# Reading a carried-in state through 128x128 weights: eight matmuls with 8 streamed columns in place of eight with 128 and two gathers

## The reference, cut to what matters

```python
G = jnp.cumsum(blk(g), axis=3)
qg = qc * jnp.exp(G)
kg = kc * jnp.exp(-G)
A = jnp.where(causal, jnp.einsum('bhncd,bhnsd->bhncs', qg, kg), 0.0)
o_intra = jnp.einsum('bhncs,bhnsv->bhncv', A, vc)
...
o_inter = jnp.einsum('bhncd,nbhdv->bhncv', qg, s_prev)
o = (o_intra + o_inter).transpose(0, 2, 3, 1, 4).reshape(b, n * c, H, dv)[:, :L]
```

## Time and profile before

| | |
|---|---|
| median of 3 runs | 2112.25 us (2110.99 to 2112.82) |
| profiled execution, its own time | 2110.99 us |
| its span | 2109.4 us |
| the eight rounds | about 220 us to 900 us of the span, 87 to 88 us each |
| PE busy | 2029.4 us, 96% |
| PE matmul records | 14632 |
| DVE busy | 1047.8 us, 50% |
| ACT busy | 809.1 us, 38% |

### The profile page before, as it was taken

How to read it: one execution, slowest core, us unless ns; L and a number is a source line. 1 busy time by engine, 2 the same in 40 slices (tenths; PEclk the granted TensorE clock), 3 DMA queues, 4 the chain that set the end, 5 groups by cost and what they waited for, 6 DMA issues and landing times.

```text
span 2109.4 us, 38265 instructions
## 1 busy us (share of the span) xinstructions
PE 2029.4 (96%) x14632; PEld 1905.8 (90%) x14632; DVE 1047.8 (50%) x1333; ACT 809.1 (38%) x1068; POOL 74.9 (4%) x119
## 2 busy tenths in 40 slices
PE   7999999999999999879998899999999999999996
PEld 6999878888788788679998899999999999999996
DVE  6344545546555355455445744444444445445445
ACT  5333444434444344244334433333323333445442
POOL 1001010010100101000000000000000000000000
PEclk9999999999999999999999999999999999999998
DMA  7776797988879889865643354444444444443441
GB/s 252 169 239 213 292 346 275 343 301 321 339 283 349 302 309 341 291 225 184 226 160 109 111 170 149 149 148 140 148 150 159 149 149 142 149 149 131 167 139 50
DMA packets 123910, 444.00 MB, mean 210 GB/s; under 512 B 14517, under 2 KB 18645, under 8 KB 123792
## 3 DMA queue, kind: packets, MB, share of 16 engines
q1 hardware_dynamic: 113888, 403.78, 53.6%
q0 software_dynamic: 9968, 39.48, 6.4%
HBM read 423.28 MB, written 22.54 MB: 211 GB/s over the span
## 4 chain that ended last, share of the span: by engine, by line
PE 88%; DVE 6%; ACT 2%; issue 2%; DMA 2%; DVEq 0%; ACTq 0%; SPq 0%
PE ps L395 22%; PE ps L397 21%; PE ps L396 21%; PE ps L1520 4%; PE ps L1521 4%; PE ps L1522 4%; PE ps L821 3%; PE ps L855 2%; DMA raw<-w_in 1%; DVE w_lo L354 1%; ACT w_hi L377 1%; DVE s L548 1%; DVE h_lo L1456 0%; DVE mixed L1449 0%; PE ps L651 0%
## 5 line engine op out<-in xcount | busy, mean ns | idle before, releaser
L354 DVE TENSOR_TENSOR w_lo<-raw,w_hi 128x1024 fp32r<-128x1024 f32 x416 | 504.9, 1223 | 593.1 <-ACT w_hi L349 290.2
L395 PE MATMUL ps<-x_hi,w_hi 128*128 128x320 f32 x1408 | 447.4, 318 | 17.3 <-DVE w_lo L354 11.1
L395 PE MATMUL ps<-h_hi,w_hi 128*128 128x320 f32 x1408 | 435.7, 309 | 13.8 <-issue 7.1
L396 PE MATMUL ps<-x_hi,w_lo 128*128 128x320 f32 x1408 | 436.2, 310 | 0.0
L397 PE MATMUL ps<-x_lo,w_hi 128*128 128x320 f32 x1408 | 435.8, 310 | 0.0
L396 PE MATMUL ps<-h_hi,w_lo 128*128 128x320 f32 x1408 | 434.6, 309 | 0.0
L397 PE MATMUL ps<-h_lo,w_hi 128*128 128x320 f32 x1408 | 434.5, 309 | 0.0
L349 ACT ACTIVATE w_hi<-raw 128x1024 fp32r<-128x1024 f32 x240 | 250.5, 1056 | 412.0 <-PE ps L397 411.8
L395 PEld LDWEIGHTS ps<-x_hi,w_hi 128*128 128x128 f32 x1408 | 265.8, 189 | 64.0 <-issue 38.7
L395 PEld LDWEIGHTS ps<-h_hi,w_hi 128*128 128x128 f32 x1408 | 265.0, 188 | 16.1 <-DVE h_lo L1456 7.7
L396 PEld LDWEIGHTS ps<-x_hi,w_lo 128*128 128x128 f32 x1408 | 266.0, 189 | 0.0
(11 more groups left out here) (282 smaller groups left out, 2270.4 us busy)
## 6 DMA issues: line engine op xcount, KB each, us to landing
raw<-w_in SPq DMA_DIRECT2D x176, 512.0 KB, 7.2
raw<-w_up SPq DMA_DIRECT2D x176, 512.0 KB, 3.3
raw<-ck SPq DMA_DIRECT2D x128, 512.0 KB, 6.0
raw<-cv SPq DMA_DIRECT2D x128, 512.0 KB, 7.1
raw<-w_dn SPq DMA_DIRECT2D x88, 512.0 KB, 3.3
raw<-w_out SPq DMA_DIRECT2D x32, 512.0 KB, 4.1
uT<-stage POOLq DMA_DIRECT2D x14, 640.0 KB, 3.7
raw<-w_hg SPq DMA_DIRECT2D x16, 512.0 KB, 4.4
```

The costliest lines, as they stand in the source:

```text
L354: dve.tensor_tensor(w_lo[half][:, :], raw[slot][:, :], w_hi[half][:, :].bitcast(F32), ALU.subtract).then_inc(lo_ready, 1)
L395: pe.matmul(out, wh[:, c, m, :], xh(c), start=first, stop=False)
L396: pe.matmul(out, wl[:, c, m, :], xh(c), start=False, stop=False)
```

## The change

The eight matmuls of L624 swap their operands and move. The state `s0[:, b, :]` (128x128) becomes the stationary operand and the 8 columns of `qg` of sample b the streamed one, so that the result is 8 columns of bank 4, added there at once. They stand in q = 7, ahead of the wait for `o_att`. The matmuls with `pick`, ACT's copy of `o_s0`, the buffers `o_s0` and `pick` and the load of `pick` go. PE's step `o` is now done in q = 7. At q = 5 PE waits for ACT's `pdt` and DVE's `st4` apart, and DVE's q = 6 waits for `ds`.

```diff
-        h_pe = Steps(sem("h_pe"), "scores vk i_t kd_t a ds o_s0 pd_t pv o ds_s", 1)
-        h_act = Steps(sem("h_act"), "ef tok lg eG p i_tok kd_tok pdt o_s0 o_att", 1)
+        h_pe = Steps(sem("h_pe"), "scores vk i_t kd_t a ds pd_t pv o ds_s", 1)
+        h_act = Steps(sem("h_act"), "ef tok lg eG p i_tok kd_tok pdt o_att", 1)
...
-        CONSTS = 16 * 12
+        CONSTS = 16 * 11
...
-                act.wait_ge(h_vec.sem, h_vec.at(h, "st4"))
-                h_act.done(act.activation(o_s0[:, :, :], ps[:, 6, 2 * DV:4 * DV].rearrange("p (g d) -> p g d", g=2),
-                                          ACT.Copy), "o_s0")
...
             if q == 6:
-                dve.wait_ge(h_pe.sem, h_pe.at(h, "o_s0"))
+                dve.wait_ge(h_pe.sem, h_pe.at(h, "ds"))
...
-                for b in range(NB):
-                    g, j = b // 4, b % 4
-                    t0, at = SEQ + 32 * g, (2 + g) * DV
-                    ins = pe.matmul(ps[32 * j:32 * j + 32, 6, at:at + DV], qg[:, t0:t0 + 32], s0[:, b, :],
-                                    start=True, stop=True)
-                h_pe.done(ins, "o_s0")
...
             if q == 5:
-                pe.wait_ge(h_act.sem, h_act.at(h, "o_s0"))
+                pe.wait_ge(h_act.sem, h_act.at(h, "pdt"))
+                pe.wait_ge(h_vec.sem, h_vec.at(h, "st4"))
...
-                for g in range(2):
-                    t0 = SEQ + 32 * g
-                    ins = pe.matmul(ps[:, 4, t0:t0 + 32], o_s0[:, g, :], pick[:, :], start=False, stop=True,
-                                    skip_group_check=True)
+            if q == 7:
+                for b in range(NB):
+                    t0 = SEQ + NQ * b
+                    ins = pe.matmul(ps[:, 4, t0:t0 + NQ], s0[:, b, :], qg[:, t0:t0 + NQ],
+                                    start=False, stop=True, skip_group_check=True)
                 h_pe.done(ins, "o")
-            if q == 7:
                 pe.wait_ge(h_act.sem, h_act.at(h, "o_att"))
```

More of the change, by code:

```diff
@@ L117, in build @@
 def build(nc, xT, ck, cv, st, pt, w_in, w_hg, w_da, w_out, w_up, w_dn, nrm, hgw, lbl, lamv,
-          table, c_ident, c_scan, c_causal, c_own, c_pick, c_hot, c_coef,
+          table, c_ident, c_scan, c_causal, c_own, c_hot, c_coef,
           y_T, k_T, v_T, h_p, h_s):
@@ L161, in build @@
         own = sb("own", [CHUNK, NB // 2], F32, at_in)
-        pick = sb("pick", [P, 32], F32, at_in)
         lb_t = sb("lb_t", [P, 8, HEADS], F32, at_in)
@@ L212, in build @@
         kd_tok = sb("kd_tok", [P, 3, P], F32, at_h)
-        o_s0 = sb("o_s0", [P, 2, DV], F32, at_h)
         i_own = sb("i_own", [CHUNK, NB // 2, DV], F32, at_h)
@@ L1733, in _ @@
                              (ident[:], c_ident), (hot[:], c_hot), (tab[0:32, :], table), (scan_keep[:], c_scan),
-                             (causal[:], c_causal), (own[:], c_own), (pick[:], c_pick), (hg_w[:], hgw), (pages[:], pt)):
+                             (causal[:], c_causal), (own[:], c_own), (hg_w[:], hgw), (pages[:], pt)):
                 pool.dma_start(dst, src).then_inc(const_landed, 16)
@@ L1810 @@
         hot[32 if dist < 0 else bucket(dist), j] = 1
-    pick = np.zeros((P, 32), np.float32)
-    for b in range(4):
-        for t in range(NQ):
-            pick[32 * b + NQ * b + t, NQ * b + t] = 1
     coef = np.zeros((P, 2), np.float32)
@@ L1833 @@
         "c_own": (i[:, None] // NQ % 4 == np.arange(NB // 2)[None, :]).astype(np.float32),
-        "c_pick": pick, "c_hot": hot, "c_coef": coef,
+        "c_hot": hot, "c_coef": coef,
     }
```

## The result

The changed kernel is slower: median 2124.94 us of six runs (2121.10 to 2127.61), against 2111.40 us of the six runs of before beside it, a ratio of 1.0062 (95% interval 1.0050 to 1.0075), or +13.1 us (+10.6 to +15.8). The prediction said +5.6 us, 2118, with 2121 as its upper end. The sign is right, and the measured slowdown is more than twice the forecast one.

What follows compares the result with a forecast made beforehand. PE, busy 2029.4 of 2109.4 us, was taken as the bound. Net +0.74 us per head over 8 heads is +5.9, less 0.3 for shorter waits: +5.6 on the median 2112.25, said as 2118 us, range 2113.5 to 2121.

Steps and rivals of the forecast that it cites:

- Removed, 1.05 us a head: On PE, the eight `o_s0` matmuls (0.58 us) and two `pick` matmuls (0.47 us) go, together 1.05 us per head.
- Added, 16 x 112 ns = 1.79 us: On PE, eight f32 matmuls with 128x128 weights and 8 streamed columns, 16 records at 112 ns, 1.79 us per head.
- a pitch of 105 ns: Low end of the forecast's 105 to 125 ns spacing of the added records, put at +4.9 us.
- The overhead rule: About 60 cycles per matmul; by it alone the added matmuls cost 0.4 us per head and the time is 2107.
- It all reaches the end, `turn`'s wait stays: PE's +0.74 us per head reaches the end; the 1.25 us wait for softmax at `turn` moves with PE, unchanged.
- DVE's copy of `o`: L572 now waits for the eight matmuls' end, with 0.3 us to spare and idle time behind; costs nothing.
- The 0.3 us allowed for a shorter wait for late weights: A slower PE lets its wait for a split with a late granule shrink: -0.3 us in all.
- The failed step: In the rounds PE runs at 2.4 GHz, granted clock 1.00, and nothing in the change takes enough away to alter that.
- Rivals: Streamed columns set the price, 7 in 100; hidden in `turn`'s wait, 5; partly cheaper load, 10; no overlap, 8.
- "no overlap": Added loads wait for short matmuls to drain: 4.8 us a head, +30 us, 2142; chance 8 in 100 above 2121.

Runs made afterwards that it cites:

- e4: The changed kernel without the eight 8-column matmuls (the samples' part of o left out): 2103.44 us against 2111.72 us for the kernel before.
- e3: The changed kernel with 64 streamed columns instead of 8 in each of the eight matmuls, into bank 5, sum into o left out: 2119.14 us, ratio 1.0033.
- e2_split: The changed kernel with four of the eight matmuls at the end of q = 6 and four in q = 7: 2118.11 us, ratio 1.0033.
- e6_most: The kernel before, with DVE finding the maximum ahead of the update of s0 in the seven full rounds: 2103.77 us, ratio 0.9967.
- r1: The changed kernel again, nothing altered, profiled once more: 2121.82 us.
- e10: The changed kernel with the eight matmuls directly behind ds_s instead of directly ahead of it: 2124.04 us, ratio 1.0063.
- r3_after: The changed kernel again, nothing altered, the third of three more profiles: 2125.45 us.
- e8_d0: The changed kernel with the eight matmuls behind granule D0, ahead of the scores of group 3, instead of behind granule 7: 2119.13 us, ratio 1.0035.

## Why the prediction was wrong, point by point

- *Removed, 1.05 us a head*: right as PE's work. The distances from `ds` to `pd_t` and from L628 to granule 7 lost 0.58 and 0.47 us (255.62-255.26 = 0.36 us from the last L628 to the granule, as the last L638 to `pick` had the earlier trace rows), and e4 measured -8.3 us.
- *Added, 16 x 112 ns = 1.79 us*: right, 1.77. (In the range, a pitch of 105 ns gives +4.7 with the 0.3 taken off, and not +4.9; nothing hangs on it.) The choice of the row with the same weight shape over the row with the same 8 columns was the sound one; e3 shows why.
- *The overhead rule* of the Trainium skill's page TensorEngine Tiling (Instruction Overhead), about 60 cycles for a short matmul, did not give the time here: 16 records would take an estimated 0.4 us by it and took 1.77. The advice of the same page of the Trainium skill (When to Use Tiling), to swap a short streamed side into 32-column groups, holds: that form took 0.58 us and its two `pick` matmuls 0.47, and undoing it is what costs 0.74 a head.
- *It all reaches the end, `turn`'s wait stays*: right. 13.1 us before and after, 4.3 in the last round. DVE's copy of `o` never waited in the seven full rounds; in the last it waited 0.6 us, and PE's wait at `turn` there did not grow. The 0.3 us allowed for a shorter wait for late weights did not come: 1.7 us at `w_lo` before and after.
- *The failed step* is in the first paragraph of the prediction: "PE runs at the higher of its two levels there, 2.4 GHz, and nothing in this change takes enough away from it to alter that". The prediction took PE's busy time for its work. Busy time did not fall: it is 2.80 of 2.80 us in the stretch ahead of the dip. But PE was busy with 16 loads of weights with 8 columns behind each, and then with a quarter of the rows. Four dips of 1.6 us, 6.3 us, are the missing term. With it the sum is 5.9 + 6.3 = 12.2 us, on the median 2111.4 + 12.2 = 2123.6 for 2124.9 measured. The medians say the same: the changed kernel is 6.8 us above e2_split, which has the same work and no dip.
- The Trainium skill's page TensorE: Matmul & The Clock Gate (HAM oscillation) ties such a fall to gaps in which PE waits for data. By that rule alone the clock would have stayed up, since the stretch has no gap, and the time would have been 2117 to 2118 us. One trace shows a fall of the kind the page describes, behind e6_most's wait of 2.30 us. But the traces go beyond it: in the changed kernel the clock fell with PE busy throughout.
- *Rivals*: none named a fall of the clock. The time lies where "no overlap" had it (above 2121), but by accident: the added matmuls are as quick as forecast, and the time is lost in the granule behind them.
- *The last round.* The two profiles also differ where before had its own half clock, at `turn` and the values. 13 us of either:

```profile
876.00:889.00 13.00, 8.50 (x69) 5.57 (x73) 2.55 (x7) 5.34 (x7) 1.94 (x3) 0.61 0.81 273
```

```profile
887.00:900.00 13.00, 8.40 (x85) 6.01 (x85) 2.65 (x7) 5.34 (x7) 1.81 (x3) 0.87 0.86 291
```

  After has the higher mean clock there (0.87 against 0.61), and from `turn` to the first product of the branch projections it took 22.9 us (890.49 to 913.42) against 24.7 (879.39 to 904.08). That is -1.8 us which no step of mine foresaw; the stages behind give 1.4 us of it back. It depends on where the stretches fall and is not counted on.

Left open: why the dips fall in every second round in most profiles. The seven full rounds are alike in PE's work, and in r1 it went 0, 2, 4, 5, in e10 0, 3, 5; no experiment touched this. And the profiles do not place all of the difference between the medians. The profiled executions of the two kernels are 10.8 us apart and the medians 13.5. The changed kernel's median is 3.1 us above its profiled execution, before's 0.4 above its own. In r3_after, which took 2125.45 us, the surplus lay ahead of the first head; whether it does so in the other runs is not shown.

## What to carry to other kernels

Price a matmul with 128-column f32 weights by its weight loads, 0.22 us for the two, however few columns it streams. Then look at the stretch as a whole: PE can be 100% busy and yet do so little per microsecond that its clock is halved behind it, so keep a run of such matmuls apart from its like (in halves, as e2_split did, or between matmuls with more work, as in e8_d0), or leave it in a form that packs the array, as before. In a profile, read the granted clock of the 3 to 4 us behind such a stretch, round by round; over the whole span it moved only from 0.987 to 0.986.

## What the runs showed of the hardware that was not expected

- The granted clock fell to half (0.52 over the stretch) for 3.4 us behind 1.77 us of 8-column matmuls and 1.06 us of 32-row ones, with PE busy all the time, in four of seven rounds; with 64 columns in the same place, in none; with 3.6 us of 8-column matmuls in all seven, four of them for 6.8 us. Behind a wait of 2.30 us in e6_most it fell as well, for 3.4 us, once.
- 8 or 64 streamed columns behind a 128x128 f32 weight load cost the same within 0.05 us per 16 records (1.77 and 1.82 us).
